# MLP's second products by channel block and tile by tile, and attention's products with v over the next head's steps

## The reference

```python
s = jnp.einsum('bqgrd,btgd->bgrqt', qi, k) * scale     # 8 query heads, 2 kv heads, width 128
p = jax.nn.softmax(s, axis=-1)
return jnp.einsum('bgrqt,btgd->bqgrd', p, v)
...
h = layer_norm(x) * (1 + sc2) + sh2
ff = jnp.square(jax.nn.relu(h @ p['w_mlp1'] + p['b_mlp1'])) @ p['w_mlp2'] + p['b_mlp2']   # 1024 -> 4096 -> 1024
x = layer_norm(ALPHA * x + g2 * ff, p['ln2_g'], p['ln2_b'])
```

## Time and profile before

| | |
|---|---|
| median of 3 runs | 1797.61 us (1793.8 to 1803.71) |
| the profiled execution | 1791.86 us, its span 1790.2 us |
| mean granted clock of TensorE | 0.952 of full speed |
| TensorE busy | 1619.5 us, 90% of the span |
| VectorE, ScalarE busy | 1026.0 and 674.6 us |
| attention, first transposes to the next stage | 909.4 to 1033.9 us |
| MLP, last unit of round 1 to the last second product | 1330.2 to 1770.4 us |

### The profile page before, as it was taken

One profiled execution on the slowest core, in us unless ns is written; L12 is line 12 of the kernel. 1 busy time (PEld: TensorE's weight loads), 2 busy tenths in 40 slices (PEclk: granted clock), 3 DMA queues, 4 the chain that ended last, 5 costly groups with the idle time before them and its releaser, 6 DMA issues.

```text
span 1790.2 us, 27388 instructions
## 1 busy us (share of the span) xinstructions
PE 1619.5 (90%) x11141; PEld 1528.4 (85%) x11141; DVE 1026.0 (57%) x1409; ACT 674.6 (38%) x1145; POOL 99.2 (6%) x155
## 2 busy tenths in 40 slices
PE   4699999889999898898889899999899999999995
PEld 2599998889999898898755499999899999999995
DVE  5466666664856368987655453436863342432467
ACT  4544444334355246766445443323521121111210
POOL 1000012110011100000000000000000000000000
PEclk9799999989999899999899999999999999999998
DMA  9334445532385766876440144335122222113121
GB/s 317 102 124 139 138 145 170 170 116 94 112 295 153 254 228 182 260 250 203 139 175 24 47 159 162 115 121 183 48 71 65 70 79 70 54 67 101 66 71 59
DMA packets 159748, 241.58 MB, mean 135 GB/s; under 512 B 8048, under 2 KB 126560, under 8 KB 156576
## 3 DMA queue, kind: packets, MB, share of 16 engines
q1 hardware_dynamic: 136464, 171.45, 29.4%
q0 software_dynamic: 12304, 47.72, 7.1%
q10 hardware_dynamic: 10880, 20.97, 4.4%
HBM read 195.06 MB, written 45.06 MB: 134 GB/s over the span
## 4 chain that ended last, share of the span: by engine, by line
PE 75%; DVE 13%; ACT 7%; issue 3%; DMA 1%; SPq 0%; ACTq 0%; DVEq 0%
PE acc L821 60%; PE tp L821 12%; DVE arena L1972 2%; ACT arena L1604 2%; PE tp L1203 1%; DVE wlo L1872 1%; DVE arena L2125 1%; ACT whi L1378 1%; DMA arena<-in_w_mod 1%; PE tp L904 1%; DVE wlo L1923 1%; DVE arena L2127 1%; DMA y_nat<-arena 1%; ACT arena L1390 0%; ACT whi L1741 0%
## 5 line engine op out<-in xcount | busy, mean ns | idle before, releaser
L821 PE MATMUL acc<-hh,whi 128*128 128x322 f32 x1152 | 305.6, 327 | 22.7 <-DVE wlo L1872 7.2
L821 PE MATMUL acc<-hl,whi 128*128 128x322 f32 x1152 | 299.4, 321 | 0.0
L821 PE MATMUL acc<-hh,wlo 128*128 128x322 f32 x1152 | 297.5, 320 | 0.0
L821 PEld LDWEIGHTS acc<-hh,whi 128*128 128x128 f32 x1152 | 209.9, 199 | 25.3 <-issue 15.2
L1872 DVE TENSOR_TENSOR wlo<-raw,whi 128x2048 fp32r<-128x2048 f32 x76 | 173.9, 2290 | 93.9 <-ACT whi L1378 93.6
L1378 ACT ACTIVATE whi<-raw 128x2048 fp32r<-128x2048 f32 x76 | 144.8, 1907 | 207.6 <-PE acc L821 207.6
L821 PEld LDWEIGHTS acc<-hl,whi 128*128 128x128 f32 x1152 | 210.8, 198 | 0.0
L821 PEld LDWEIGHTS acc<-hh,wlo 128*128 128x128 f32 x1152 | 210.1, 198 | 0.0
L821 PE MATMUL acc<-whi,fh 128*128 128x256 f32 x640 | 183.1, 286 | 15.4 <-DVE fl L2478 15.4
L821 PE MATMUL acc<-whi,hh 128*128 128x256 f32 x640 | 183.8, 287 | 0.0
L821 PE MATMUL acc<-wlo,fh 128*128 128x256 f32 x640 | 183.1, 286 | 0.0
(11 more groups left out here) (282 smaller groups left out, 2833.7 us busy)
## 6 DMA issues: line engine op xcount, KB each, us to landing
raw<-in_w_in SPq DMA_DIRECT2D x38, 1024.0 KB, 6.9
raw<-in_w_mlp SPq DMA_DIRECT2D x32, 1024.0 KB, 5.4
arena<-in_w_mod SPq DMA_DIRECT2D x24, 1024.0 KB, 6.3
arena<-decay_sums_t ACTq DMA_DIRECT2D x40, 512.0 KB, 5.4
arena<-xs_nat SPq DMA_DIRECT2D x8, 1024.0 KB, 8.3
raw<-in_w_ssd_o SPq DMA_DIRECT2D x8, 1024.0 KB, 6.2
y_nat<-arena POOLq DMA_DIRECT2D x6, 1024.0 KB, 7.4
arena<-y_nat SPq DMA_DIRECT2D x6, 1024.0 KB, 6.2
```

What stands on the lines that cost most here:

```text
L821: return pe.matmul(out, l, r, start=first, stop=last)
```

## The change

- **MLP, rounds 1 to 3.** `first_two` runs the first two units (tiles 0 and 1 of output block 0) over channel blocks 0 to 6, tile 0 waiting for each `ff` by itself, and then block 7 of both. The other 18 units follow as before, in two banks.
- **MLP, last round.** It is taken out of TensorE's loop, which now has two rounds. `last_products` goes through `LAST`, an order in which tiles are finished one after another, with four banks of `acc`. For it, the third and fourth weight blocks are split into buffers of their own (`w3h`, `w3l`, over `hh` and `hl`), which ScalarE and VectorE do as soon as they can. On VectorE each tile is aggregated, normalised and released for its store as soon as its four units are in, with one unit between the variance and the passes.
- **Attention.** `values(h)` is dealt out over the four steps of the next head, 1, 2, 1 and 2 of its six products, ahead of that step's transposes. `att_out` and `att_lower` of the head stand one head later, in the step n % 4 == 0. `values(7)` goes ahead of the transposes of the last step.

```diff
+        over_h = lambda h: h[:].rearrange("p k t -> p (k t)")[:, 0:2 * KT * BW].rearrange("p (b k n) -> p b k n", b=2, k=KT)
+        w3h, w3l = over_h(hh), over_h(hl)
...
@@ -364,6 +368,9 @@
         assert F_END > 0
+        V_PARTS = ((0,), (1, 2), (3,), (4, 5))
...
@@ -373,6 +380,11 @@
         OUT = [(0, 0), (1, 0), (2, 0), (0, 1), (1, 1), (0, 2), (0, 3), (1, 2), (1, 3), (2, 1), (2, 2), (2, 3)]
         OUT += [(t, b) for t in range(3, NT) for b in range(4)]
         TURN = {10: 0, 14: 1, 17: 2}
+        LAST = [(0, 0), (1, 0), (2, 0), (0, 1), (1, 1), (0, 2), (0, 3), (1, 2), (1, 3), (2, 1), (2, 2), (2, 3)]
+        LAST += [(t, b) for t in range(3, NT) for b in range(4)]
+        WHOLE = {max(i for i, u in enumerate(LAST) if u[0] == t): t for t in range(NT)}
         def block_done(p):
@@ -1203,34 +1215,35 @@
                     last = pe.transpose(tp[:, j // 4, (j % 4) * P:(j % 4 + 1) * P], pr[:, u, j * P:(j + 1) * P], ident)
                 last.then_inc(pt_turned["sem"], step(pt_turned))
-            def values(h):
-                step(pvf)
-                if some(pvf, 2):
-                    pe.wait_ge(pvf["sem"], value(pvf, 2))
+            def values(h, js=range(6)):
                 o = tp[:, 2 + h % 2]
-                if h == 0:
-                    pe.wait_ge(s["av_in"], 16 * 3)
+                if js[0] == 0:
+                    step(pvf)
+                    if some(pvf, 2):
+                        pe.wait_ge(pvf["sem"], value(pvf, 2))
+                    if h == 0:
+                        pe.wait_ge(s["av_in"], 16 * 3)
+                    pe.wait_ge(s["p_copied"], 4 * (h + 1) if h < HQ else N_SCORE + h - HQ + 1)
                 if h < HQ:
-                    pe.wait_ge(s["p_copied"], 4 * (h + 1))
-                    for j in range(6):
+                    for j in js:
                         v = (vn[:, 1 + j] if j < 4 else vc[:, j - 4])[:, (h // R) * HD:(h // R + 1) * HD]
                         last = mul(o, v, pT[:, h % 2, j], j == 0, j == 5)
                 else:
                     g = h - HQ
-                    pe.wait_ge(s["p_copied"], N_SCORE + g + 1)
                     last = mul(o, vn[:, 0, g * HD:(g + 1) * HD], pT[:, h % 2, 0])
-                last.then_inc(pv["sem"], step(pv))
+                if js[-1] == 5:
+                    last.then_inc(pv["sem"], step(pv))
             scores(0)
             scores(1)
             for n in range(N_SCORE + HKV):
                 if n + 2 < N_SCORE + HKV:
                     scores(n + 2)
+                if 4 <= n < N_SCORE:
+                    values(n // 4 - 1, V_PARTS[n % 4])
+                if n == N_SCORE + 1:
+                    values(HQ - 1)
                 turn_p(n)
-                if n % 4 == 1 and 4 < n < N_SCORE:
-                    values(n // 4 - 1)
-            values(HQ - 1)
             values(HQ)
             values(HQ + 1)
@@ -1332,12 +1345,48 @@
             ff = count(s["ff_ok"])
+            def mlp_products(out, t, wh, wl, ks, waits=False):
+                for k in ks:
+                    if waits:
+                        pe.wait_ge(ff["sem"], due(ff))
+                    for m, w in ((fh, wh), (fh, wl), (fl, wh)):
+                        last = mul(out, m[:, k, tok(t):tok(t) + P], w[:, k], k == 0 and w is wh and m is fh, k == KT - 1 and m is fl)
+                return last
+            def first_two(outs, backs):
+                pe.wait_ge(lo["sem"], due(lo))
+                for t in range(2):
+                    step(free)
+                    pe.wait_ge(free["sem"], value(free, backs[t]))
+                    mlp_products(outs[t], t, whi[:, 0], wlo[:, 0], range(KT - 1), t == 0)
+                for t in range(2):
+                    mlp_products(outs[t], t, whi[:, 0], wlo[:, 0], [KT - 1], t == 0).then_inc(ready["sem"], step(ready))
             def second_products():
-                for n in range(KT):
-                    pe.wait_ge(ff["sem"], due(ff))
+                first_two([acc[:, 0, 0:BW], acc[:, 2, 0:BW]], (2, 2))
                 for b in range(4):
-                    pe.wait_ge(lo["sem"], due(lo))
-                    n_block(b % 2, fh, fl)
+                    if b:
+                        pe.wait_ge(lo["sem"], due(lo))
+                    for t in range(2 if b == 0 else 0, NT):
+                        step(free)
+                        pe.wait_ge(free["sem"], value(free, 2))
+                        mlp_products(acc[:, 2 * ((NT * b + t) % 2), 0:BW], t, whi[:, b % 2], wlo[:, b % 2],
+                                     range(KT)).then_inc(ready["sem"], step(ready))
+            def last_products():
+                blocks = [(whi[:, 0], wlo[:, 0]), (whi[:, 1], wlo[:, 1]), (w3h[:, 0], w3l[:, 0]), (w3h[:, 1], w3l[:, 1])]
+                seen = 1
+                first_two([acc[:, 0, 0:BW], acc[:, 1, 0:BW]], (2, 3))
+                for i in range(2, 4 * NT):
+                    t, b = LAST[i]
+                    if b == seen:
+                        pe.wait_ge(lo["sem"], due(lo))
+                        seen += 1
+                    step(free)
+                    pe.wait_ge(free["sem"], value(free, 4 if i > 3 else i + 1))
+                    mlp_products(acc[:, i % 4, 0:BW], t, *blocks[b], range(KT)).then_inc(ready["sem"], step(ready))
             pe.wait_ge(s["h2_ok"], 3)
@@ -1360,10 +1409,13 @@
             for n in range(4, KT):
                 mlp_unit(n)
             second_products()
-            with rounds(pe, 3, (lo, 8), (ready, KT + 4 * NT), (free, KT + 4 * NT), (ff, KT)):
+            with rounds(pe, 2, (lo, 8), (ready, KT + 4 * NT), (free, KT + 4 * NT), (ff, KT)):
                 for n in range(KT):
                     mlp_unit(n)
                 second_products()
+            for n in range(KT):
+                mlp_unit(n)
+            last_products()
         @block.scalar
         def _(act):
@@ -1720,11 +1772,11 @@
             for n in range(N_SCORE + HKV):
                 if n + 1 < N_SCORE + HKV:
                     exps(n + 1)
+                if n % 4 == 0 and n >= 8:
+                    att_out(n // 4 - 2)
                 if n == N_SCORE + 1:
                     att_out(HQ - 1)
                 probs_out(n)
-                if n % 4 == 1 and 4 < n < N_SCORE:
-                    att_out(n // 4 - 1)
                 if n - 1 in GATED:
                     q = GATED[n - 1]
                     squares(0, q, z0[:, q * 512:(q + 1) * 512])
@@ -1836,7 +1888,7 @@
             relu, sq = count(s["relu_ok"]), count(s["square_ok"])
-            def mlp_round(last_round):
+            def first_squares():
                 for n in range(KT):
                     act.wait_ge(relu["sem"], due(relu))
                     act.activation(fh[:, n], hf2[:, n % 2], ACT.Square).then_inc(sq["sem"], step(sq))
@@ -1844,16 +1896,19 @@
                     if n % 2 == 1:
                         act.wait_ge(ready["sem"], value(ready))
                         split_hi(n // 2 % 2)
+            with rounds(act, 3, (ready, KT + 4 * NT), (hi, 8), (raws[0], 4), (raws[1], 4), (relu, KT), (sq, KT)):
+                first_squares()
                 for b in range(4):
                     step(ready, NT)
-                    if b < 2 or not last_round:
-                        act.wait_ge(ready["sem"], value(ready))
-                        split_hi(b % 2)
-            with rounds(act, 3, (ready, KT + 4 * NT), (hi, 8), (raws[0], 4), (raws[1], 4), (relu, KT), (sq, KT)):
-                mlp_round(False)
-            mlp_round(True)
-            roots(mv[:, :, 2])
+                    act.wait_ge(ready["sem"], value(ready))
+                    split_hi(b % 2)
+            first_squares()
+            for b in range(2):
+                act.wait_ge(raws[b]["sem"], due(raws[b]))
+                act.activation(w3h[:, b], raw[:, b], ACT.Copy).then_inc(hi["sem"], step(hi))
+            for t in range(NT):
+                roots(mv[:, t, 2:3])
         @block.vector
         def _(dve):
@@ -2281,8 +2336,8 @@
                 probabilities(n)
                 if n + 2 < N_SCORE + HKV:
                     maxima(n + 2)
-                if n % 4 == 1 and 4 < n < N_SCORE:
-                    att_lower(n // 4 - 1)
+                if n % 4 == 0 and n >= 8:
+                    att_lower(n // 4 - 2)
                 if n in GATED:
                     gated(0, GATED[n])
             for h in range(HQ - 1, HQ + 2):
@@ -2465,7 +2520,7 @@
             sqb = row[:, 0:TP]
             dve.wait_ge(s["h2_ok"], NT)
-            def mlp_round(i, last_round):
+            def relu_round(i):
                 for n in range(KT):
                     dve.wait_ge(ready["sem"], due(ready))
                     r = hf2[:, n % 2]
@@ -2478,33 +2533,56 @@
                     dve.tensor_tensor(fl[:, n], sqb, fh[:, n].bitcast(F32), ALU.subtract).then_inc(ff["sem"], step(ff))
                     if n % 2 == 1:
                         split_lo(n // 2 % 2)
+            def second_round():
```

(52 more changed lines are left out.)

## The result

The changed kernel takes 1745.08 us (median of 4 runs, 1743.12 to 1750.14) against 1795.7 (4 runs, 1787.74 to 1803.71): a ratio of 0.9732, 95% interval 0.9704 to 0.9759. The prediction was 1748. The profiled execution took 1745.69, its span 1744.0, so 46.2 us less than the span of before.

What follows compares the result with a forecast made beforehand. TensorE carries three quarters of the chain, so removing its idle or low-clock time, or work behind its last product, pays. Gains of 14.5 + 1.8 + 15.8 + 17.5 = 49.6 us take the median from 1797.61 to 1748, range 1738 to 1764.

Steps and rivals of the forecast that it cites:

- The waits ahead of the second products: MLP rounds 1 to 3: 42 matmuls cover the wait for `fl`, a 1.6 us bank wait remains; gain 14.5 us.
- T: End of unit 7, the last first-product unit of an MLP round, from which the forecast counts its times.
- The loop: TensorE's MLP loop: one turn less saves 1.71 us and leaving it costs 0; gain given as 1.8 us.
- The last round: MLP's last round: four banks, four of five tiles' passes hidden under products, end at T + 65.8; gain 15.8 us.
- Attention: Products with v dealt out, att_out and att_lower later: heads of 13.1 us instead of 14.35; gain 17.5 us.
- B: Last round: VectorE takes TensorE's place as the bound, gain 8 us instead of 15.8, time 1756; chance 0.12.
- C: MLP rounds 1 to 3: the new 1.6 us wait still drops the clock, costing 8 us, time 1756; chance 0.09.
- D: Attention stays bound by the softmax, gain 5 us instead of 17.5, time 1760; chance 0.10.
- E: Attention's TensorE work, mixed with short waits, stays at half clock: slower, 1839 us; chance 0.02.

Runs made afterwards that it cites:

- written-out version: The changed kernel with four banks in rounds 1 to 3 too and TensorE's two rounds written out instead of looped: 1741.92 us, ratio 0.9690.
- its variant: The kernel before with only att_out and att_lower moved to the next head's step n % 4 == 0: 1792.12 us, ratio 1.0001.

## Why the prediction was right, point by point

- **The waits ahead of the second products** were mapped rightly. The 42 matmuls covered `fl`, the next thing late was the bank, and TensorE went on at T + 7.2 (7.25 forecast). The term was 14.5 and measured 13.7; it used 57.9 us a round, and 58.1 to 58.3 came.
- **The loop.** There is one turn less, and leaving the loop cost nothing (no idle time ahead of the last round's first unit). The 2.2 us for 1.8 come from the turn that is left, which took 1.4 us here; turns varied. The Trainium skill (Runtime: NRT & Kernel Launch, Instruction fetch mechanics) says that fetching is sequential and that a taken branch to a page that is not loaded waits for its fetch; idle time at each turn (1.40 to 2.05 us), and none at the exit or in the written-out version, agree with it in kind.
- **The last round.** Block 3 came 0.7 us before it was due (0.3 forecast) and the end at T + 65.2 (65.8). The last unit was ready at T + 56.8 (56.4 forecast) and was begun at once, where T + 57.4 was forecast. VectorE was free 1.1 us sooner than forecast: block 3's lower part ended 0.4 us sooner, and a finished tile's aggregate, variance, reciprocal and passes took 3.2 us beside its units rather than 3.3, so no backlog was left where I had counted 1 us. Behind it 8.4 us came, as forecast.
- **Attention.** The size was right (16.9 of 17.5), and its reasoning in part wrong. The step that failed is the sentence that the 0.85 us "arises because `att_lower` stands in VectorE's queue". Moving it alone gave 0.7 us in the whole stretch and 0.3 a head. What gains is that the products stand ahead of the transposes, and that they are short pieces. The size was in part luck. The last transposes of a latent tile ended 98.1 us after step 0, where the forecast's 1007.5 means 99.5; from there to the projection it was 10.9 us and not 8.9, in part for a wait of 0.99 us ahead of the context's transposes, which the forecast lacks. The two errors nearly cancel. The forecast's own terms also sum to 1016.9 and not 1016.4 for the start of the projection, so to 17.0 rather than 17.5.
- **The rivals.** The range, 1738 to 1764, held the times of B, C and D too, so the time alone does not tell them from the forecast; the stretches do. B did not come: VectorE had 0.54 us to spare at the end. C did not come for this wait: the clock stayed at 1.00 after all 25 such waits for a bank (1.41 to 1.52 us) seen in the traces. D, a softmax bound, did not come with the pieces dealt out; where only `att_lower` is moved, the chain of a head does run through VectorE and ScalarE. E had no sign.
- **The median.** It is 50.6 us less (48.1 by the ratio), 49.6 forecast. The forecast started from 1797.61, the median of three runs before; a fourth made it 1795.7. The profiled pair shows only 46.2, since 2.9 us were lost before attention. I take that as scatter (below): of the kernel before and its variant only two executions were profiled, with step 0 at 908.0 and 908.1, and the eleven others lie on both sides of that, so a small effect of the change is not excluded.

## What to carry to other kernels

When a trace names the instruction that an engine waits for, ask what the releasing engine was doing in the microseconds before: an idle releaser can mean that work reaches it too late, and then moving the named instruction helps little. A long product that needs nothing new belongs in short pieces between the steps of a chain that crosses engines, each behind the work that feeds the other engines. In a final stage, order the units so that whole tiles are finished evenly, and write the queue's schedule out by hand with durations from the trace: the last round came out within 0.6 us of it.

## What the runs showed of the hardware

- **Idle time and the clock.** TensorE's granted clock fell to 0.50 (1.2 GHz) after all 12 idle stretches of 3.7 to 4.0 us ahead of second products, and after none of the 25 waits for a bank of 1.41 to 1.52 us. After the 14 turns of the MLP's loop, 1.40 to 2.05 us idle, it fell twice, after 1.78 and 1.95 us. The two units behind the turn took 16.12 us in that second case, where they take 14.55 behind a turn at the full clock:

```profile
1504.00:1505.00 1.00, 0.82 (x4) 0.83 (x5) 0.78 (x1) 0.18 (x1) 0.00 (x0) 0.79 0.00 0
1505.00:1506.00 1.00, 1.00 (x6) 1.00 (x5) 1.00 (x1) 0.00 (x0) 0.00 (x0) 0.50 0.05 16
...
1508.00:1509.00 1.00, 1.00 (x8) 1.00 (x8) 0.00 (x0) 0.00 (x0) 0.00 (x0) 1.00 0.77 208
```

  The length of one stretch does not decide it alone. In the tail of attention three waits of 1.25, 1.39 and 1.44 us stand close together in the kernel before, and the clock fell about the end of the last; in the run with attention as before the same three (1.25, 1.40, 1.44) left it at 1.00. The idle 3.36 us ahead of step 0 left the clock at 1.00 in 11 of 13 executions. A wait under 2 us is thus not safe, and removing the turn removes a chance as well as its idle time. I had expected only the long waits to cost twice.
- **The scatter between executions.** Much of it arises before attention. The two profiles of the changed kernel differ by 7.2 us up to step 0 (910.86 and 903.70), and by 4.9 behind it the other way, 2.6 of them in attention's first steps at the low clock. In the kernel before, rounds of the first projection last 41.2 us (114.28 to 155.49) or 38.1 (237.73 to 275.84), each with an idle stretch of 2.3 us ahead of its transposes, and over 8 us behind them the clock reads 0.67 in the one and 1.00 in the other:

```profile
116.00:124.00 8.00, 8.00 (x40) 7.98 (x40) 0.33 (x2) 1.62 (x2) 0.87 (x1) 0.67 0.60 192
239.00:247.00 8.00, 8.00 (x56) 7.98 (x56) 0.43 (x3) 0.46 (x2) 0.87 (x1) 1.00 0.67 209
```

  Which rounds are short differs from execution to execution. That the 2.3 us waits are what lets the clock fall there was read from the traces and not tried.
